# Both output projections of a two-block layer kernel turned token-major

## The chip, the cores and the metric

One core of one Trainium2 chip runs the whole program in one launch. The metric is the device time of that core in microseconds (us). The engines are TensorE (PE: matmuls, and its weight loads PEld), VectorE (DVE), ScalarE (ACT), GpSimd (POOL) and SyncE (SP), which issues nearly all transfers. P is 128, T (tokens) and D (features) are 1024, KT = TT = 8 tiles of 128, and HALF is 512.

## The reference, cut to what matters

Two transformer-like blocks follow each other. Block 1 ends in a gated residual and a final norm; block 2 norms its input, ends its mixer in a normed residual, and then runs a feed-forward part (FFN):

```
# block 1: merged is (T, D), the sum of three gated branches; gt_l comes from silu(c) @ w_ada + b_ada
x_new = x + gt_l * (merged @ w_out)
x2    = rmsnorm(x_new, final_g)                   # y * rsqrt(mean(y*y) + 1e-6) * g
# block 2
u  = rms_norm(x2, norm_mix_pre)                   # goes into the mixers (the first is hgrn)
h  = x2 + rms_norm(merged_2 @ w_out_2, norm_mix_post)
u  = rms_norm(h, norm_ffn_pre)
h  = h + rms_norm((silu(u @ w_gate) * (u @ w_up)) @ w_down, norm_ffn_post)
```

Everything is float32. Each product of the kernel is made of three matmuls of "high" and "low" parts: x = x_hi + x_lo with x_hi a rounded copy (fp32r), and x_hi w_hi + x_lo w_hi + x_hi w_lo is summed in PSUM.

## The kernel before, in words

**Feature-major sums.** Activations lie with features on the partitions: `h_hi`, `h_lo` and `acc` are [128, 8 feature tiles, 1024 tokens]. A product's output tile is 128 features by 512 tokens. Its stationary operand is a 128x128 block of the weights and its moving operand 512 tokens of `h`.

**Weights.** Weights arrive in chunks of 512 KB in two slots of `raw` (SP, `load_chunk`). ACT rounds a chunk into `w_hi` (`round_chunk`, L303), POOL subtracts to get `w_lo` (`rest_chunk`, L310), and `split` counts the halves that are ready. `used` counts chunks that PE has finished with.

**The merge ahead of each projection** writes the merged sum to `acc`, two feature tiles per turn of a loop, in the order 6, 7, 4, 5, 2, 3, 0, 1. PE makes a gate product and a branch product, ACT the sigmoid, DVE multiplies (L1197) and POOL adds into `acc` (L1166).

**`project_first` (L1558).** J = 16 pieces, each of one feature tile and one half of the tokens; the eight chunks of `w_out` are fetched twice, once for each half of the tokens. ACT and DVE first split the merged sum into high and low (L1622, L1667). For each piece PE turns four 128x128 blocks of x to feature-major (`turn`, L1743, from `res`, into which the merge loaded x), makes 24 matmuls, and DVE multiplies by the gate column `gate_t` and adds x (L1674). ACT squares twice (L1634, L1635), DVE sums the squares over the feature tiles (L1681), PE sums them over the partitions with one-column matmuls (`stats`, L1761), DVE and POOL make the two inverse roots (L1601), DVE writes a diagonal, and PE spreads it over the partitions (`spread`, L1769). The normed tiles (`normed`, L1706) are split again into `h_hi` and `h_lo`. x_new goes to DRAM (`keep`), and the inverse root of the first norm stays in `kept_rstd`.

**`project_second` (L1812)** does the same with `w_out_2`, but has two norms one behind the other (the product's, then the sum's), so it has four rounds of sum over partitions, inverse root and spread, and it first rescales the x_new that it has fetched back to get x2 (`rescale`, L1956). `add_residual` (L1838), `square_x` (L1901), `add_square_x` (L1978) and `weighted` (L1968) make the second norm.

**What follows.** Both end with `half_ahead`: products of the next stage's first two chunks with the first half of the tokens, 48 matmuls in four parts, between the last steps. The other half waits for `h_done`, the last `h_lo`. `ffn_and_output` (L3461) adds the residual at its end token-major, so PE turns `res` there (`residual_tile`, L3695) and ACT copies it (L3582). DVE adds the last products (L3621), POOL makes the inverse root (L3552), DVE scales (L3629) and DVE or POOL add the residual (L3511).

**What sets the order.** Each engine has its instructions in the order written, a queue of its own, and waits on semaphores between. Nothing is planned at run time. The same kind of product as the new one already stands in the FFN (`down_tile`, L3657 to L3659): a 128-token tile is stationary, a row of the weight matrix 512 wide moves, and the two output halves lie in different PSUM banks.

## Time and profile before

| | |
|---|---|
| three runs, us | 3081.94, 3085.1, 3087.03 (median 3085.1) |
| the profiled execution's own time, us | 3083.83 |
| its span in the profile, us | 3082.1 |
| PE busy | 2934.9 us, 95% of the span |
| DVE, ACT, POOL busy | 44%, 31%, 33% |
| mean granted TensorE clock | 0.979 |

The span runs from the program's first instruction to its last on the core. A busy matmul is not a matmul at its peak: their ends are modelled, and in a dense stream each overlaps the next, so the distance from start to start is what counts.

### The profile page before, as it was taken

Reading aid. Unit: us, or ns where it says so; the run is one execution under the profiler, and the core shown is the slowest. Engines: PE = TensorE matmul, PEld = TensorE weight load, DVE = VectorE, ACT = ScalarE, POOL = GpSimd, SP = SyncE. Lnnn points to the kernel's source line nnn. Section 1 sums busy time; section 2 is a strip of 40 time slices with the busy share of each in tenths; the row PEclk is TensorE's granted clock in tenths of the full one; section 3 lists DMA queues with packets and bytes.
Section 4 is the critical chain, followed back from the end, with each engine's and each line's share of the span. In section 5 each row is a group of like instructions: output and inputs, shape, how many; then the busy total and the mean of one; then the engine's idle time right before and its main releaser. Section 6 shows DMA issues by size and latency. Waiting matters only on the chain.

```text
span 3082.1 us, 40975 instructions
## 1 busy us (share of the span) xinstructions
PE 2934.9 (95%) x15675; PEld 2365.4 (77%) x15675; DVE 1352.4 (44%) x2203; ACT 956.7 (31%) x1574; POOL 1016.1 (33%) x801
## 2 busy tenths in 40 slices
PE   5999989999999999999989999989878999999998
PEld 3788778888888877788677888758666888888886
DVE  5244430111011035544379999850663324324325
ACT  4344532222233244332453222352332111111113
POOL 3534312233333345222122333304554223223223
PEclk8999999999999999999999999999988999999999
DMA  5211021111112122111011111102220111111111
GB/s 206 51 39 39 18 79 54 48 48 41 54 50 92 51 92 86 51 36 53 24 37 37 46 46 51 39 37 70 76 62 28 48 48 48 48 48 48 48 48 75
DMA packets 261468, 169.42 MB, mean 55 GB/s; under 512 B 23604, under 2 KB 250605, under 8 KB 260205
## 3 DMA queue, kind: packets, MB, share of 16 engines
q1 hardware_dynamic: 259997, 162.65, 17.5%
q10 hardware_dynamic: 1360, 5.24, 0.4%
q8 instruction: 75, 1.23, 0.2%
q14 instruction: 36, 0.29, 0.0%
HBM read 159.41 MB, written 8.45 MB: 54 GB/s over the span
## 4 chain that ended last, share of the span: by engine, by line
PE 87%; DVE 6%; issue 2%; ACT 2%; POOL 1%; DMA 1%; SPq 0%; POOLq 0%; DVEq 0%; ACTq 0%
PE ps L326 69%; PE ps L3658 3%; PE ps L3657 3%; PE ps L3659 2%; PE ps L983 1%; PE ps L997 1%; DVE score L3076 1%; DVE ssq L1944 1%; DVE h_lo L1934 1%; PE ps L2480 1%; PE ps L3402 1%; PE ps L3392 1%; DMA rows<-in_norm_ffn_post 0%; PE ps L969 0%; PE ps L1523 0%
## 5 line engine op out<-in xcount | busy, mean ns | idle before, releaser
L326 PE MATMUL ps<-h_hi,w_hi 128*128 128x512 f32 x2864 | 1139.1, 398 | 35.3 <-DVE h_lo L1934 10.1
L326 PE MATMUL ps<-h_lo,w_hi 128*128 128x512 f32 x2864 | 1123.3, 392 | 0.0
L326 PE MATMUL ps<-h_hi,w_lo 128*128 128x512 f32 x2864 | 1122.3, 392 | 0.0
L310 POOL TENSOR_TENSOR w_lo<-raw,w_hi 128x512 fp32r<-128x512 f32 (+2 forms) x556 | 658.2, 1205 | 1296.9 <-ACT w_hi L303 1296.7
L326 PEld LDWEIGHTS ps<-h_hi,w_hi 128*128 128x128 f32 x2864 | 542.2, 189 | 157.9 <-issue 19.6
L326 PEld LDWEIGHTS ps<-h_hi,w_lo 128*128 128x128 f32 x2864 | 542.0, 189 | 116.4
L326 PEld LDWEIGHTS ps<-h_lo,w_hi 128*128 128x128 f32 x2864 | 542.6, 189 | 111.0 <-issue 1.0
L303 ACT ACTIVATE w_hi<-raw 128x512 fp32r<-128x512 f32 (+2 forms) x556 | 288.3, 567 | 865.2 <-PE ps L326 701.5
L3607 DVE TENSOR_TENSOR act<-gate,ps 128x1024 f32<-128x1024 f32 x22 | 26.9, 1221 | 446.1 <-PE ps L326 446.1
L3616 DVE TENSOR_TENSOR acc<-acc,ps 128x1024 f32<-128x1024 f32 x160 | 195.4, 1221 | 28.6 <-PE ps L3659 28.6
L1197 DVE TENSOR_TENSOR part<-sig,ps 128x1024 f32<-128x1024 f32 x40 | 48.6, 1215 | 339.1 <-PE ps L326 285.5
L3168 DVE MATCH_REPLACE8 score<-best,score 128x384 f32<-128x384 f32 (+2 forms) x192 | 165.8, 876 | 0.0
L3169 DVE MAX8 best<-score 128x8 f32<-128x384 f32 (+2 forms) x192 | 155.7, 878 | 1.1
L3658 PE MATMUL ps<-w_lo,act_hi 128*128 128x512 f32 x352 | 140.3, 399 | 0.0
L3657 PE MATMUL ps<-w_hi,act_hi 128*128 128x512 f32 x352 | 139.4, 396 | 0.2 <-POOL w_lo L310 0.2
L3659 PE MATMUL ps<-w_hi,act_lo 128*128 128x512 f32 x352 | 138.1, 392 | 0.0
L3547 POOL TENSOR_TENSOR act_lo<-act,act_hi 128x1024 fp32r<-128x1024 f32 x21 | 50.6, 2408 | 187.2 <-ACT act_hi L3578 187.2
L1166 POOL TENSOR_TENSOR acc<-acc,part 128x1024 f32 x40 | 96.9, 2422 | 0.0
L3578 ACT ACTIVATE act_hi<-act 128x1024 fp32r<-128x1024 f32 x22 | 23.3, 1061 | 217.5 <-DVE act L3607 217.5
L3573 ACT ACTIVATE gate<-ps 128x1024 f32<-128x1024 f32 x22 | 22.6, 1027 | 211.1 <-PE ps L326 211.1
L3657 PEld LDWEIGHTS ps<-w_hi,act_hi 128*128 128x128 f32 x352 | 66.1, 188 | 17.2 <-POOL w_lo L310 0.6
L3659 PEld LDWEIGHTS ps<-w_hi,act_lo 128*128 128x128 f32 x352 | 66.1, 188 | 15.7
(434 smaller groups left out, 3406.5 us busy)
## 6 DMA issues: line engine op xcount, KB each, us to landing
raw<-in_w_in SPq DMA_DIRECT2D x88, 512.0 KB, 4.0
raw<-in_w_ffn_gate_up SPq DMA_DIRECT2D x44, 512.0 KB, 3.8
raw<-in_w_out SPq DMA_DIRECT2D x32, 512.0 KB, 3.7
raw<-in_w_gate SPq DMA_DIRECT2D x32, 512.0 KB, 4.1
raw<-in_w_ffn_down SPq DMA_DIRECT2D x22, 512.0 KB, 3.5
w_ada<-in_w_ada SPq DMA_DIRECT2D x8, 1024.0 KB, 10.7
x_tok<-in_x ACTq DMA_DIRECT2D x4, 1024.0 KB, 14.0
residual_gate<-in_w_ada SPq DMA_DIRECT2D x8, 512.0 KB
```

Of the source, the lines that this page charges most:

```text
L303: act.activation(w_hi[:, s, cut], raw[:, s, cut], ACT.Copy).then_inc(rounded.sem, 1)
L310: pool.tensor_tensor(w_lo[:, s, cut], raw[:, s, cut], w_hi[:, s, cut].bitcast(F32), ALU.subtract).then_inc(split.sem, 1)
L326: last = pe.matmul(dst, w[:, chunk[0] % 2, k], x(k), start=(k == ks[0] and n == 0), stop=(k == ks[-1] and n == 2))
L1166: pool.tensor_tensor(to, to, part[:], ALU.add).then_inc(o_evicted.sem, 1)
L1197: dve.tensor_tensor(part[:], sig[:, u % 2], ps[2 * (u % 2) + 1][:], ALU.mult)\
L3168: top_steps.done(dve.match_replace(part(b), best[:, j], part(b), TAKEN) if marking else dve.max(best[:, j], part(b)))
L3169: dve.max(best[:, j], part(b)))
L3547: pool.tensor_tensor(act_lo[:, f % 2], act32[:], act_hi[:, f % 2].bitcast(F32), ALU.subtract)\
L3616: dve.tensor_tensor(acc[:, t], acc[:, t], outs[t][:], ALU.add).then_inc(o_evicted.sem, 1)
L3657: pe.matmul(dst[:, c:c + HALF], act_hi[:, f % 2, tokens], w[0], start=first, stop=False)
L3658: pe.matmul(dst[:, c:c + HALF], act_hi[:, f % 2, tokens], w[1], start=False, stop=False)
L3659: last = pe.matmul(dst[:, c:c + HALF], act_lo[:, f % 2, tokens], w[0], start=False, stop=final)
```

## The change

`project_first` and `project_second` are written anew around one helper, `row_products`. The output tile is now 128 tokens by 1024 features (two banks of PSUM), the stationary operand a 128x128 block of the merged sum, the moving operand half a row block of the weight matrix. Norms, gains and residual then act on rows whose tokens lie on the partitions.

- **Weights:** `Rows` loads eight row blocks (128 rows of 4 KB) once, into `raw` and a second pair of slots, `raw_x`. Six of them are kept split in `rows_hi` and `rows_lo`. ACT rounds, and DVE, not POOL, subtracts.
- **Order:** token tiles 0 to 2 are worked on together, row block by row block in the order in which the merge finishes its tiles; the split of their 384 columns comes first (`first_tokens`), the other 640 later (`other_tokens`). Tiles 3 to 7 follow one by one, 48 matmuls each.
- **Per tile:** DVE `add`, a norm over the free axis (ACT square with its accumulator, DVE `mean`, POOL power, DVE `normed`), PE `turn` (eight 128x128 transposes into `ps3`), ACT `out_high`, DVE `out_low`.
- **Residual:** x comes token-major into the space of `acc` once that is split, in four parts of 1 MB. x2 itself (gain included) is stored and fetched back; `kept_rstd`, `rescale` and the FFN's `residual_tile` go.
- **Gate:** the gate of the residual is made as a row on all partitions (`gate_row`, two matmuls 512 wide in the first merge) instead of a column per feature tile.

The core of the diff:

```
+            def weights(self, m):
+                return [wide_row(x[:, m]) for x in (w_hi, w_lo)] if m < 2 else [self.high[:, m - 2], self.low[:, m - 2]]
+        def row_products(pe, rows, gates, turn, ahead, t_last=TT - 1):
+            def step(t, m, c, n, last=False):
+                x, w = ((h_hi, 0), (h_hi, 1), (h_lo, 0))[n]
+                return pe.matmul(ps[t % 3][:, c:c + HALF], tile_of(x, t)[:, ROW_ORDER[m]], rows.weights(m)[w][:, c:c + HALF],
+                                 start=(m == 0 and n == 0), stop=last and n == 2)
+            pe.wait_ge(*gates[1])
+            for m in range(6):
+                pe.wait_ge(hi_ready.sem, hi_ready.at(m + 1))
+                for t in range(FEW):
+                    for half, c in enumerate((0, HALF)):
+                        if t == 0:
+                            rows_ready(m, half)
+                        step(t, m, c, 0)
+                        step(t, m, c, 1)
+                pe.wait_ge(lo_ready.sem, lo_ready.at(m + 1))
+                for t in range(FEW):
+                    for c in (0, HALF):
+                        step(t, m, c, 2)
+            ...
+            for t in range(FEW, TT):
+                pe.wait_ge(evicted.sem, evicted.at(t - 2))
+                for m in range(KT):
+                    if m == 4 and t < 5:
+                        turn(2 * t - 6)
+                    for c in (0, HALF):
+                        for n in range(3):
+                            done = step(t, m, c, n, m == KT - 1)
+                ...
+                done.then_inc(o_ready.sem, 1)
+                turn(2 * t - 5 if t < 5 else t - 1)
+            pe.wait_ge(evicted.sem, evicted.at(TT - 1))
+            ahead(pe, KT, 0, 0)
+            ahead(pe, KT, 0, 1)
+            pe.wait_ge(evicted.sem, evicted.at(TT))
+            ahead(pe, KT, 1, 0)
+            turn(TT - 1)
+            ahead(pe, KT, 1, 1)
+        # project_first, ACT
+                    sum_high(act, rows, acc, tile_added)
+                    squares(0)
+                    squares(1)
+                    keep(0)
+                    squares(2)
+                    keep(1)
+                    keep(2)
+                    out_high(0)
+                    squares(3)
+                    out_high(1)
+                    ...
+                    for t in range(4, TT):
+                        squares(t)
+                        out_high(t - 1)
+                        if t == TT - 2:
+                            round_chunk(act, KT, 0, 0)
+                            round_chunk(act, KT + 1, 0, 0)
+                        keep(t)
+        # project_first, DVE
+                    def add(t):
+                        x, y = tmp[:, t % FEW], x_of(t)
+                        ...
+                        dve.tensor_tensor(x, ps[t % 3][:], gate_row[:], ALU.mult).then_inc(evicted.sem, 1)
+                        ...
+                        dve.tensor_tensor(x, x, y, ALU.add).then_inc(y_ready.sem, 1)
+                        ...
+                        dve.tensor_tensor(y, x, final_row[:], ALU.mult).then_inc(y_ready2.sem, 1)
+                    sum_low(dve, rows, acc)
+                    add(0)
+                    add(1)
+                    mean(0)
+                    normed(0)
+                    add(2)
+                    mean(1)
+                    normed(1)
+                    mean(2)
+                    normed(2)
+                    out_low(0)
+                    add(3)
+                    out_low(1)
+                    ...
+                    for t in range(4, TT):
+                        add(t)
+                        out_low(t - 1)
+                        mean(t)
+                        normed(t)
+                    out_low(TT - 1)
+        # PE, both projections
+                    def turn(t):
+                        pe.wait_ge(h_ready.sem, h_ready.at(t + 1))
+                        pe.wait_ge(o_evicted.sem, o_evicted.at(t))
+                        for k in range(KT):
+                            last = pe.transpose(ps[3][:, k * P:k * P + P], tmp[:, t % FEW, k * P:k * P + P], ident[:])
```

The hgrn stage now starts its first load ahead of its wait for `h_done`, and its POOL waits for the stored x2 before its first `rest_chunk`.

## Rows read from the trace of the kernel before

**Rows 1.** The page: the chain that ended last, share of the span by engine.

```profile
PE 87%; DVE 6%; issue 2%; ACT 2%; POOL 1%; DMA 1%; SPq 0%; POOLq 0%; DVEq 0%; ACTq 0%
```

**Rows 2.** Stretches: us; PE, PEld, DVE, ACT, POOL busy; clock; DMA share; GB/s.

```profile
1102.60:1232.00 129.40, 117.56 (x534) 94.88 (x532) 67.31 (x92) 60.03 (x109) 69.67 (x49) 0.96 0.30 96
2178.69:2342.66 163.97, 126.79 (x533) 100.60 (x533) 119.29 (x147) 55.85 (x99) 80.91 (x60) 0.87 0.20 58
```

**Rows 3.** Waits in 2160 to 2340 us: total us, times, longest.

```profile
PE ps L2057 <- DVE ssq_x L1978: 11.1, 1, 11.1
PE ps L326 <- DVE h_lo L1934: 10.1, 5, 4.9
```

**Rows 4.** PE in order of time: the first matmul behind each projection.

```profile
1232.00 0.77 PE L326 MATMUL ps<-h_hi,w_hi 128*128 128x512 f32 x1 [4.19 <-DVE h_lo L1582]
...
2342.66 0.76 PE L326 MATMUL ps<-h_hi,w_hi 128*128 128x512 f32 x1 [9.63 <-DVE h_lo L1832]
```

**Rows 5.** PE in order of time: dense streams, first and last matmul of each.

```profile
2196.09 0.39 PE L326 MATMUL ps<-h_hi,w_lo 128*128 128x512 f32 x1
...
2204.25 0.39 PE L326 MATMUL ps<-h_hi,w_lo 128*128 128x512 f32 x1
...
2343.22 0.63 PE L326 MATMUL ps<-h_lo,w_hi 128*128 128x512 f32 x1
...
2347.06 0.63 PE L326 MATMUL ps<-h_lo,w_hi 128*128 128x512 f32 x1
...
3007.74 0.39 PE L3657 MATMUL ps<-w_hi,act_hi 128*128 128x512 f32 x1
...
3015.45 0.39 PE L3657 MATMUL ps<-w_hi,act_hi 128*128 128x512 f32 x1
```

**Rows 6.** PE in order of time: eight transposes and the next matmul.

```profile
3047.31 1.03 PE L3695 MATMUL ps<-ident,res 128*128 128x128 f32 x8
3048.10 0.48 PE L3657 MATMUL ps<-w_hi,act_hi 128*128 128x512 f32 x1
```

**Rows 7.** DVE in order of time.

```profile
1102.88 1.22 DVE L1197 TENSOR_TENSOR part<-sig,ps 128x1024 f32<-128x1024 f32 x1 [15.28 <-PE ps L326]
1104.02 9.26 DVE L1667 TENSOR_TENSOR h_lo<-acc,h_hi 128x512 fp32r<-128x512 f32 x8
...
1115.25 0.68 DVE L1667 TENSOR_TENSOR h_lo<-acc,h_hi 128x512 fp32r<-128x512 f32 x1
...
2200.84 1.78 DVE L1934 TENSOR_TENSOR h_lo<-acc,h_hi 128x512 fp32r<-128x512 f32 x1
...
3049.45 1.28 DVE L3629 SCALAR_TENSOR_TENSOR acc<-acc,rstd,gate 128x1024 f32<-128x1024 f32 x1
...
3056.01 2.61 DVE L3629 SCALAR_TENSOR_TENSOR acc<-acc,rstd,gate 128x1024 f32<-128x1024 f32 x1
```

**Rows 8.** ACT in order of time.

```profile
1102.86 1.15 ACT L303 ACTIVATE w_hi<-raw 128x512 fp32r<-128x512 f32 x2 [0.25 <-PE ps L326]
...
3046.11 1.03 ACT L3582 ACTIVATE res<-ps 128x1024 f32<-128x1024 f32 x1 [2.73 <-PE ps L3695]
3047.03 1.05 ACT L3593 ACTIVATE act<-acc 128x1024 f32<-128x1024 f32 x1
3047.98 0.19 ACT L3593 ACTIVATION_READ_ACCUMULATOR act<-acc 128x1 f32 x1
```

**Rows 9.** POOL in order of time.

```profile
1104.72 2.83 POOL L1166 TENSOR_TENSOR acc<-acc,part 128x1024 f32 x1
...
2240.99 1.02 POOL L1853 TENSOR_TENSOR rs<-var,power 128x4 f32<-128x4 f32 x1 [6.35 <-DVE var L1961]
...
3054.63 0.54 POOL L3552 TENSOR_TENSOR rstd<-var,power 128x1 f32<-128x1 f32 x1 [1.94 <-DVE var L3625]
```

**Rows 10.** The page, DMA issues: count, KB each, us to landing.

```profile
raw<-in_w_out SPq DMA_DIRECT2D x32, 512.0 KB, 3.7
x_tok<-in_x ACTq DMA_DIRECT2D x4, 1024.0 KB, 14.0
```

More of the change, by code:

```diff
@@ L1240, in _ @@
                         pe.wait_ge(evicted2.sem, evicted2.at(U * N - 1))
-                        for d in range(KT):
-                            last = pe.matmul(ps[1][:, d:d + 1], residual_gate[:, 0, d * P:d * P + P], ones[:, 0:1],
-                                             start=True, stop=True)
+                        for c in (0, HALF):
+                            last = pe.matmul(ps[1][:, c:c + HALF], ones[:], residual_gate[:, 0, c:c + HALF], start=True, stop=True)
                         last.then_inc(sum_ready.sem, 1)
@@ new lines, in sum_low, with low @@
+        def sum_low(dve, rows, acc):
+            def low(cut, n, high_done, done):
+                dve.wait_ge(high_done.sem, high_done.at(n + 1))
+                dve.tensor_tensor(cut(h_lo, n), cut(acc, n), cut(h_hi, n).bitcast(F32), ALU.subtract).then_inc(done.sem, 1)
+            for n in range(KT):
+                low(first_tokens, n, hi_ready, lo_ready)
+                if n == 0:
+                    dve.wait_ge(split.sem, half_after(split, 0, 1, 0, 0))
+                if n < 2:
+                    rows.rest(dve, n + 1)
+                if n == 5:
+                    rows.rest(dve, 3)
+            rows.rest(dve, 4)
+            for m in range(5, KT):
+                rows.rest(dve, m)
+                for n in range(2 * (m - 5), 2 * (m - 5) + 2):
+                    low(other_tokens, n, y_hi, lo_ready2)
+            for n in range(6, KT):
+                low(other_tokens, n, y_hi, lo_ready2)
@@ new lines, in _ @@
+                @block.tensor
+                def _(pe):
+                    def turn(t):
[3 more added lines that the diff above has]
+                            last = pe.transpose(ps[3][:, k * P:k * P + P], tmp[:, t % FEW, k * P:k * P + P], ident[:])
+                        last.then_inc(transposed.sem, 1)
+                    row_products(pe, rows, gates, turn, half_ahead)
@@ new lines, in out_high @@
+                    def out_high(t):
+                        act.wait_ge(transposed.sem, transposed.at(t + 1))
+                        act.activation(tile_of(h_hi, t), by_feature(ps[3]), ACT.Copy).then_inc(y_ready3.sem, 1)
+                    sum_high(act, rows, acc, tile_added)
+                    square(0, 0)
+                    square(0, 1)
+                    square(1, 0)
+                    square(0, 2)
+                    square(1, 1)
+                    square(1, 2)
+                    out_high(0)
@@ L1930, in _ @@
+                    square(0, 3)
+                    out_high(1)
+                    square(1, 3)
+                    out_high(2)
+                    for t in range(4, TT):
+                        square(0, t)
+                        out_high(t - 1)
+                        square(1, t)
+                        if t == TT - 2:
+                            round_chunk(act, KT, 0, 0)
+                            round_chunk(act, KT + 1, 0, 0)
+                    out_high(TT - 1)
                 @block.vector
@@ L2016, in _ @@
+                    sum_low(dve, rows, acc)
+                    dve.wait_ge(side_loaded.sem, side_loaded.at(2))
+                    mean(0, 0)
+                    add(0)
+                    mean(0, 1)
+                    add(1)
+                    mean(1, 0)
                     normed(0)
+                    mean(0, 2)
+                    add(2)
+                    mean(1, 1)
                     normed(1)
-                    rest(dve, 1)
-                    evict(12)
+                    mean(1, 2)
@@ L2036, in _ @@
-                    for n in range(KT, J):
-                        normed(n)
-                        if n > KT and n % 2 == 0:
-                            rest(dve, n - 1)
-                    rest(dve, J - 1)
+                    out_low(0)
+                    mean(0, 3)
+                    add(3)
+                    out_low(1)
+                    mean(1, 3)
+                    normed(3)
+                    out_low(2)
+                    for t in range(4, TT):
+                        mean(0, t)
+                        add(t)
+                        out_low(t - 1)
+                        mean(1, t)
+                        normed(t)
@@ L2055, in stats @@
-                    def stats(src):
-                        for t in range(4):
-                            last = pe.matmul(ps[3][:, t:t + 1], src[:, t * P:t * P + P], ones[:, 0:1], start=True, stop=True)
-                        last.then_inc(scores.sem, 1)
-                    def spread(dst, n, scales):
-                        pe.wait_ge(biased.sem, biased.at(n + 1))
-                        pe.matmul(dst, ones[:], scales, start=True, stop=True).then_inc(pt_ready.sem, 1)
-                    pe.wait_ge(*gates[1])
```

830 lines of the change are left out of this document (300 added, 530 removed).

## The prediction

> **What bounds the kernel now.** I read the page's chain of waits first: PE holds 87% of it [rows 1], so what counts is where PE is idle, slow, or does work that the change drops. The two projections are stretches of their own in the view by windows. The first runs from 1102.60, where the merge's last product is issued, to 1232.00 us, the second from 2178.69 to 2342.66 [rows 2]. Their ends are the first matmuls that had waited for the last `h_lo` [rows 4]. Each stretch holds 384 matmuls of the projection and 48 of the next stage (`half_ahead`).
>
> A dense stream of such matmuls goes at (2204.25 - 2196.09) / 36 = 0.2267 us each [rows 5], so 432 need 97.9 us. The first projection takes 129.4 us, 31.5 over it, the second 164.0, 66.1 over it. The granted clock says the same: 0.96 and 0.87 [rows 2]. In the second, the view of waits names PE standing 11.1 us for the sum of the squares of h, and 10.1 us for splits of the merged sum, which DVE makes beside POOL [rows 3]. At its end there are two norms one behind the other, and the last wait alone is 9.63 us [rows 4]. The second stretch is where the money is.
>
> **The change part by part.** S is the moment when PE issues the first product of a projection.
>
> *Matmuls.* Their number stays: 8 token tiles x 8 row blocks x 2 halves x 3 = 384, and 48 ahead. Their pattern becomes that of `down_tile`: token tile stationary, weight row moving, the bank of PSUM changing every second or third matmul. There the step is (3015.45 - 3007.74) / 33 = 0.2336 us [rows 5]. The other end is 0.2267. I take 0.2336, the row of the same pattern: 432 x 0.2336 = 100.9 us.
>
> *Turns.* Eight turns of eight transposes take the place of one-column matmuls, spreads and, in the first projection, 16 turns of four. Eight transposes hold PE 0.79 us (3048.10 - 3047.31) [rows 6], and the next matmul starts some 0.1 late; I take 0.9, so 7.2 us. Sum per projection without a wait: 108.1 us.
>
> *The start.* Before, eight splits by DVE took 9.26 us [rows 7] and PE followed them one by one. Now PE has 108 matmuls (25.2 us) on tiles 6, 7, 4, 5, 2, 3 before it needs tiles 0 and 1. DVE is free at S + 1.5 (L1197 begins at S + 0.3 and takes 1.22 [rows 7]); then come the split of 384 columns (0.46, by 0.68 for 512) and row block 1 in two pieces of 0.6. POOL adds the last merged tile from S + 2.1 to S + 4.9 [rows 9], and DVE's two-input pieces in that time take 1.78 instead of 0.68 us [rows 7]. So block 1 is split at about S + 5.2, where PE wants its halves at S + 4.2 and S + 4.7: 0.4 us of wait. From then on POOL is idle. A block costs ACT 1.1 us [rows 8] and DVE 1.2, PE takes 4.2 over it. All of the splits, 1.2 for each block and 0.46 + 0.74 for each tile, end near S + 21.4, well before S + 34.0, when tile 3 starts. Blocks 2 to 7 arrive in 3.7 us each [rows 10], the last near S + 16, each issued as a slot comes free. In the second projection block 0 is ready only at about S + 0.3, and the waits of the start come to 0.5.
>
> *The middle, first projection.* Products 0 to 2 end at S + 28.4, 31.2 and 34.0. `add` is three ops of 1.22 with a hand-over, 3.86 us; a square with its accumulator is 1.05 + 0.19 [rows 8]; `mean` 0.3; the power lies between 0.54 (one column) and 1.02 (four) [rows 9], I take 0.7 for two; `normed` 1.28 [rows 7]. On DVE in the order written: add 0 and 1 until 36.3, normed 0 until 38.8, add 2 until 42.5, normed 1 until 45.0, normed 2 until 47.4. ACT has `keep(2)` ahead of `out_high(0)`, so that ends at 49.5 and `out_low(0)` at 50.7. But `turn(1)` needs `out_low(0)`, because there is one `ps3`, and PE arrives at 46.2, after tile 3. PE waits 4.6 us, and `turn(2)` another 0.8. Behind such a wait the clock is granted at half: 0.427 us a matmul against 0.2267, for 12 matmuls behind the wait of 9.63 us (9 steps of it in [rows 5]) and 7 behind that of 4.19. I add 7 x 0.2 = 1.4. From tile 4 on a tile is 11.2 + 0.9 us of PE against about 6.5 of DVE and 5.6 of ACT, so nothing waits.
>
> *The end, first projection.* Let T be when PE has issued the last product. From there: add 7 until T + 4.0; its second square until T + 5.2; `out_high(6)`, behind it on ACT, T + 6.3; `out_low(6)` T + 7.4; mean, power and `normed(7)` T + 10.0. PE meanwhile makes `turn(6)` and three of the four quarters ahead (0.9 + 8.4 = 9.3) and waits 0.7 for `turn(7)`. The last quarter (2.8) covers `out_high(7)` and `out_low(7)`. SP fetches the next two chunks right behind the fourth store of x2, and POOL's splits of them (2 x 2.55) lie ahead of its last power, which is needed later. Sum: 108.1 + 0.4 + 4.6 + 0.8 + 0.7 + 1.4 = 116.0 us, against 129.4. That is 13.4 saved, and 7 x 0.2 = 1.4 more, since hgrn no longer starts at half clock.
>
> *The second projection.* Both norms are chains of a square, `mean`, a power of 0.54 and one op, but `add` has two wide ops instead of three and nothing is kept, so `out_low(0)` ends at S + 47.7 where PE arrives at 46.2: 1.5 us. At the end `normed(7)` is done 8 us behind the last product and PE wants it after 9.3. Sum: 108.1 + 0.5 + 1.5 = 110.1 us against 164.0: 53.9 saved, and 12 x 0.2 = 2.4 for the FFN's first matmuls.
>
> *The FFN's end.* Eight turns leave PE and eight copies ACT. PE is not what is late there: DVE is busy from add to add, and the first square alone stands behind a copy of 1.03 us [rows 8], of which 0.6 is waiting. I take 0.6 (bounds 0 and 8 x 0.79 = 6.3).
>
> *At nothing:* the gate's row in the first merge (DVE has three more turns of that loop, 16 small matmuls become 2 wide ones); storing and fetching x2 in 4 MB each (the parts land from S + 20 on, the first is due at S + 29.7); hgrn's POOL waiting for the last store, which begins near S + 112 and has until S + 122. If a store or a part took 14.0 us like the four loads of x at the start [rows 10], x2's parts would come up to some 10 us late.
>
> Sum: 14.8 + 56.3 + 0.6 = 71.7. The profiled execution took 3083.83, which gives 3012.1; the median of the runs is 1.3 above it, so 3013.4.
>
> **Rules of the Trainium skill.** The row shows a split by DVE at 1.78 us beside POOL against 0.68 alone, and the scaling L3629 at 2.61 beside POOL's add against 1.28 [rows 7]. The Trainium skill, SBUF — State Buffer, section "Who interferes with whom", says that a VectorE instruction with two SBUF inputs blocks against a GpSimd instruction that reads SBUF. By it the splits of the weights, which were POOL's, cost DVE nothing beyond their own time, as POOL reads nothing wide after the merge's last add.
>
> **The rivals.**
> - *A second chain that paces PE* (waits in place of the sums over partitions). For it: turns are tied by one `ps3` and by the written order on ACT and DVE, and the middle already waits 4.6 us. Against it: from tile 4 on DVE has half of its time free. If hand-overs or the power cost twice what I take, each of the first turns and each end waits some 5 us more: 4 places, 20 us, 3033.
> - *Transfers late.* For it: row blocks pass through four slots, x through the space of `acc`, 14.0 us to land [rows 10]. Against: 3.7 us for the same 512 KB. 10 us: 3023.
> - *Slower than before: the half clock.* One mechanism: banks that change every two or three matmuls leave gaps in PE, the clock is granted at 1.2 GHz for both projections, and each of 768 matmuls costs 0.2 us more: 154 us, 3167. It decides from 0.09 us a matmul on, 71.7 / 768. Against: `down_tile` changes banks as often and keeps 0.2336 [rows 5], which only the 2.4 GHz level allows. [...]
> - *It doesn't do what it says:* the next stage gives it back, because its first tiles lie where the kept rows lay and it waits for them: within 0.2% of 3085.
>
> **How the numbers follow.** Forecast 3013, chance 0.76; its own range 3003 to 3023 (dense step 0.2267: - 4.6; no wait in the middle: - 6; other sizes of power and hand-over: + 8). Paced by the chain 0.11, late transfers 0.08, other partial loss 0.02, no change 0.01, half clock 0.02. Range 3001 to 3034. This kernel's runs agree within 0.2%, some 6 us, and anything inside that is "same". Faster 0.96, same 0.01, slower 0.03.
>
> **What would show it.** Right: the stretches take about 116 and 110 us at a clock near 1.0; the new matmuls stand 0.23 us apart; `h_lo` no longer releases PE at a start; one wait of some 5 us at the second turn of the first projection and 1 to 2 us in the second; no half-clock matmuls at hgrn's or the FFN's start. Wrong: PE waiting at turns from tile 4 on, DVE pieces of 1.7 us after S + 5, PE waiting for weight rows, steps of 0.43 us.

## The result and the profile after

The changed kernel takes 3011.65 us (median of 4 runs, 3009.72 to 3013.24) against 3083.52 us before (4 runs, 3080.61 to 3087.03) on the same chip: ratio 0.9766, 95% interval 0.9749 to 0.9783. The forecast was 3013 us, with a range of 3001 to 3034. The profiled execution's span is 3007.9 us (before 3082.1) at a mean clock of 0.988 (0.979).

The page's chain by engine answers to [rows 1]: PE now holds 89% of it. The two stretches, with the same columns, answer to [rows 2]:

```profile
PE 89%; DVE 5%; ACT 2%; issue 2%; POOL 1%; DMA 1%; SPq 0%; POOLq 0%; DVEq 0%; ACTq 0%
```

```profile
1102.75:1219.77 117.02, 110.60 (x497) 89.79 (x496) 74.23 (x87) 51.06 (x76) 15.22 (x20) 0.97 0.33 115
2161.20:2270.90 109.70, 108.25 (x497) 87.48 (x497) 63.76 (x79) 45.09 (x75) 18.74 (x26) 1.00 0.28 96
```

The first projection went from 129.4 to 117.0 us, the second from 164.0 to 109.7, and the second now runs at a mean clock of 1.00. The waits of PE in the changed kernel, first from 1085 to 1225 us and then from 2160 to 2300 us (total us, times, longest), answer to [rows 3]. What stood at 11.1 and 10.1 us is gone, and only five single waits are left:

```profile
PE ps L1864 <- DVE h_lo L1830: 4.4, 1, 4.4
PE ps L1864 <- DVE tmp L1825: 1.3, 1, 1.3
PE ps L1651 <- DVE w_lo L1589: 0.7, 1, 0.7
...
PE ps L2035 <- DVE h_lo L1997: 1.1, 1, 1.1
PE ps L1651 <- DVE w_lo L1589: 0.3, 1, 0.3
```

L1651 is the new product, L1864 and L2035 are the turns, L1589 DVE's split of the row blocks. The largest wait is the one in the middle of the first projection. PE in order of time around it, and what DVE and ACT did for it:

```profile
1149.09 0.39 PE L1651 MATMUL ps<-rows_hi,h_lo 128*128 128x512 f32 x1
1153.90 1.94 PE L1864 MATMUL ps<-ident,tmp 128*128 128x128 f32 x8 [4.42 <-DVE h_lo L1830]
1155.49 0.78 PE L1651 MATMUL ps<-w_hi,h_hi 128*128 128x512 f32 x1
1156.07 0.63 PE L1651 MATMUL ps<-w_lo,h_hi 128*128 128x512 f32 x1
...
1159.48 0.44 PE L1651 MATMUL ps<-w_hi,h_hi 128*128 128x512 f32 x1
```

```profile
1140.66 1.29 DVE L1825 SCALAR_TENSOR_TENSOR tmp<-acc,rstd,pre_row 128x1024 f32<-128x1024 f32 x1 [0.89 <-POOL rstd L1748]
1152.53 1.23 DVE L1830 TENSOR_TENSOR h_lo<-ps,h_hi 128x1024 fp32r<-128x1024 f32 x1 [2.12 <-ACT h_hi L1777]
```

```profile
1150.44 1.15 ACT L1773 ACTIVATE acc<-acc,rstd 128x1024 f32<-128x1024 f32 x1 [1.21 <-DVE tmp L1825]
1151.49 1.00 ACT L1777 ACTIVATE h_hi<-ps 128x1024 fp32r<-128x1024 f32 x1
```

Tile 0 is normed at 1141.95, PE turns it, but ACT reads the turned tile only at 1151.49, behind the `keep` of tile 2 (L1773), and DVE follows at 1152.53. The second turn writes to the same PSUM buffer, `ps3`, and stands for 4.42 us. Behind it the eight transposes are spread over 1.94 us instead of 1.03, and of the nine matmuls up to 1159.05 the next stands 0.58 us away once and 0.43 us eight times, which is the 1.2 GHz level.

Where the 74.2 us between the two spans went, from distances between the same places in both traces. A projection counts here from the moment when PE has issued the merge's last product:

| stretch | before, us | after, us |
|---|---|---|
| first projection | 129.4 | 117.0 |
| from it to the second | 946.7 | 941.5 |
| second projection | 164.0 | 109.6 |
| FFN, to the end | 739.4 | 737.0 |

In the second projection PE's waits came to 37.2 us before and to 1.4 after, and 38 matmuls stood 0.43 us apart before, one after. So some 43 of its 54 us are waits and the half clock behind them; the rest lies in the smaller matmuls and between them. PE hardly waited for the splits of the weights before (0.3 us in the second projection, nothing in the first), so waiting for weights that were fetched twice is not what the change took away.

### The profile page after: what moved, and what is told of

It is laid out like the page before. It is cut to its first block, busy times and chain, and to the rows that moved or that the text cites. A ratio compares the mean times of both kernels' runs of the same rounds, so it can differ in the third digit from the quotient of the medians.

```text
span 3007.9 us, 40407 instructions
## 1 busy us (share of the span) xinstructions
PE 2898.8 (96%) x15527; PEld 2336.7 (78%) x15527; DVE 1304.3 (43%) x2130; ACT 928.4 (31%) x1510; POOL 898.9 (30%) x737
## 4 chain that ended last, share of the span: by engine, by line
PE 89%; DVE 5%; ACT 2%; issue 2%; POOL 1%; DMA 1%; SPq 0%; POOLq 0%; DVEq 0%; ACTq 0%
PE ps L326 67%; PE ps L1651 5%; PE ps L3582 3%; PE ps L3584 3%; PE ps L3583 3%; PE ps L983 1%; PE ps L997 1%; DVE score L3013 1%; PE ps L2417 1%; PE ps L3339 1%; PE ps L3329 1%; DMA rows<-in_norm_ffn_post 0%; PE ps L969 0%; PE ps L1523 0%; PE ps L3350 0%
## 5 line engine op out<-in xcount | busy, mean ns | idle before, releaser
L326 PE MATMUL ps<-h_hi,w_hi 128*128 128x512 f32 x2608 | 1027.9, 394 | 4.7 <-POOL w_lo L310 4.7
L326 PE MATMUL ps<-h_hi,w_lo 128*128 128x512 f32 x2608 | 1017.2, 390 | 0.0
L326 PE MATMUL ps<-h_lo,w_hi 128*128 128x512 f32 x2608 | 1016.8, 390 | 0.0
L310 POOL TENSOR_TENSOR w_lo<-raw,w_hi 128x512 fp32r<-128x512 f32 (+1 forms) x496 | 567.5, 1166 | 1199.1 <-ACT w_hi L303 1199.1
L326 PEld LDWEIGHTS ps<-h_hi,w_hi 128*128 128x128 f32 x2608 | 490.4, 188 | 109.2 <-POOL w_lo L310 5.3
L326 PEld LDWEIGHTS ps<-h_hi,w_lo 128*128 128x128 f32 x2608 | 490.1, 188 | 103.9
L326 PEld LDWEIGHTS ps<-h_lo,w_hi 128*128 128x128 f32 x2608 | 490.7, 188 | 100.6 <-issue 0.2
L303 ACT ACTIVATE w_hi<-raw 128x512 fp32r<-128x512 f32 (+1 forms) x496 | 253.9, 561 | 861.4 <-PE ps L326 695.8
```

What stands on the lines that cost most here:

```text
L303: act.activation(w_hi[:, s, cut], raw[:, s, cut], ACT.Copy).then_inc(rounded.sem, 1)
L310: pool.tensor_tensor(w_lo[:, s, cut], raw[:, s, cut], w_hi[:, s, cut].bitcast(F32), ALU.subtract).then_inc(split.sem, 1)
L326: last = pe.matmul(dst, w[:, chunk[0] % 2, k], x(k), start=(k == ks[0] and n == 0), stop=(k == ks[-1] and n == 2))
```

## The experiments

Each comparison is with the kernel before on the same chip, whose median lay between 3080.9 and 3083.0 us. Two of the kernels below join one new projection to the old other one. Block 2's residual is then read in a form that the other stage doesn't write; apart from one memset that sets the old factor to 1, the instructions are those of the two parents.

### The two projections apart

`e_first`: the new first projection, with the old second and the old FFN end. `e_second`: the reverse.

```
 e_first:   merge, project_first, hgrn of after; project_second and the FFN's end of before
 e_second:  merge, project_first, hgrn of before; project_second and the FFN's end of after
```

> The new first projection alone; the second projection and the FFN's end are the old ones. The factor by which the old second projection brings x_new to x2 is set to 1, and x2 lies token-major where it expects feature-major, so only times are meant. Theory (each projection's gain is its own: fewer waits of PE at its start and end): the kernel before less 12.2 us of the stretch and 1.4 us of half clock at hgrn's start, some 3070 us, or 3066 if the 3.5 us of a landing in the memory stage come too. Rival (the gains need each other, since the old second projection rescales what the first has kept): 3083 or above.

Measured: 3061.53 us (3060.39 to 3062.19), ratio 0.9928 (0.9912 to 0.9943).

> The old first projection, the new second one and the new end of the FFN. The old first stores x_new feature-major and the new second takes it as x2 token-major, without the first norm's factor and gain, so only times are meant. Theory: less 54.3 us of the stretch and 2.3 us of half clock at the FFN's start, 3083.5 - 56.7 = 3026.8 us, its stretch 109 to 111 us. Rival (half of the second's gain comes from the first's part, x2 being kept instead of x_new): about 3055.

Measured: 3024.49 us (3020.30 to 3028.53), ratio 0.9805 (0.9786 to 0.9823). From the second projection's first product to the FFN's first down product it took 142.34 us, against 142.22 in the changed kernel and 199.13 before.

The second projection came out as expected: its stretch took 109.8 us. The four executions of `e_second` lie in two pairs, near 3020.6 and 3028.3 us, and the traced one is of the upper pair.

`e_first` gained more (21 us) than its projection accounts for: from the first product to hgrn's state products it took 206.5 us against 221.0 before, 14.5 less. Of the 22.2 us between the two spans another 1.6 are the first 98 us of the program, which take 95.6 to 98.3 us in the traces, whatever the kernel, and 3.6 lie at one chunk of the memory attention. The theory had those 3.6 in its second number, 3066, and the measured time is 4.5 us below even that.

The two gains apart, 21.0 and 58.0 us, add up to 79, where both changes together gave 72. The memory attention is faster in both traces (by 3.6 and 2.7 us), which counts it twice; the rest isn't settled, and is of the size by which executions differ. Neither projection needs the other's change for its gain.

### The order of `out_high` and `out_low`

`e_order` moves the two ops that read a turned tile ahead of work on later tiles, for tiles 0 to 2 of the first projection and for tile 0 of the second:

```
 # project_first, ACT                 # DVE
   keep(0)                              add(2)
+  out_high(0)                       +  out_low(0)
   squares(2)                           mean(1)
   keep(1)                              normed(1)
+  out_high(1)                          ...
   keep(2)                              normed(2)
-  out_high(0)                       -  out_low(0)
   squares(3)                        +  out_low(1)
-  out_high(1)                          add(3)
+  out_high(2)                       -  out_low(1)
   keep(3)                              ...
-  out_high(2)
```

> The new kernel with another written order in the middle of both projections: out_high(0) and out_low(0) come right behind the first turn, ahead of the squares and the keep of later tiles. Nothing is left out. Theory (the wait of 4.4 us at the second turn is the written order of ACT and DVE, not their load): the wait of the first projection falls below 1 us, with it 9 matmuls and one turn at half clock (2.5 us), and 1.1 us of the second projection: 3011.7 - 7.5 = 3004 us. Rival (DVE's load through three tiles sets it; then the wait comes back at turn 2 or 3): at most 3 us gained, 3009.

Measured: 3000.08 us (2995.29 to 3002.18), ratio 0.9729 (0.9714 to 0.9744), below the changed kernel's interval. The first projection of its trace, and DVE's two ops on turned tiles:

```profile
1100.91:1210.63 109.72, 107.72 (x497) 87.66 (x496) 74.08 (x87) 51.14 (x76) 15.21 (x20) 1.00 0.34 123
```

```profile
1143.71 1.22 DVE L1830 TENSOR_TENSOR h_lo<-ps,h_hi 128x1024 fp32r<-128x1024 f32 x1
1149.58 1.22 DVE L1830 TENSOR_TENSOR h_lo<-ps,h_hi 128x1024 fp32r<-128x1024 f32 x1
```

`out_low(0)` stands 42.8 us behind the stretch's start instead of 49.8. The stretch has 109.7 us against 117.0, at clock 1.00 against 0.97. Its 7.3 us are the wait of 4.4, the transposes and the first matmul behind it (1.59 + 0.58 instead of 0.79 + 0.32, so 1.1), and eight steps of 0.43 instead of 0.23 (1.6), 7.1 in all. The wait of 1.1 us in the second is gone too. So the order written on ACT and DVE was the cause, not a lack of time on either. The theory had 7.5 us in all, and the ratio fell by 11 us' worth; the trace is 13.5 us shorter, of which some 5 lie outside the projections, 1.8 of them in the first 98 us of the program, 2.4 between the projections and 0.7 at the FFN's end. None of that is code that `e_order` changes.

### Three tiles one by one

`e_alone` does tiles 0 to 2 each with 48 matmuls in a row, where the changed kernel goes row block by row block over all three:

```
-            for m in range(6):
-                ...
-                for t in range(FEW):
-                    for half, c in enumerate((0, HALF)):
+            for t in range(FEW):
+                for m in range(KT):
+                    if t == 0:
+                        pe.wait_ge(hi_ready.sem, hi_ready.at(m + 1))
+                        pe.wait_ge(lo_ready.sem, lo_ready.at(m + 1))
```

> The new kernel, but token tiles 0 to 2 are worked on one behind the other from the start, so PE needs all eight row blocks within the first tile. Nothing is left out. Theory (working on three tiles together is what hides the arrival, rounding and splitting of the row blocks): the eighth block is ready about 20 us after the start, so tile 0 ends near S + 22 and tile 2 near S + 43.5 in place of S + 33.4; 10 us and some half clock in each projection, 3032 to 3036 us. Rival (the start is cheap either way, since DVE splits without POOL beside it): under 5 us lost, 3016.

Measured: 3017.86 us (3014.97 to 3019.48), ratio 0.9786 (0.9770 to 0.9803). My theory missed: the loss against the changed kernel (0.9766 and 0.9759 in two series) is 6 to 8 us, and the rival's 3016 was nearer. The intervals of the ratios overlap, so the loss rests on the traces: 1.3 us more from the first projection to hgrn's state products, 7.4 more from the second to the FFN's first down product. Its waits (total, times, longest), first projection and then second:

```profile
PE ps L1651 <- DVE h_lo L1629: 2.1, 1, 2.1
PE ps L1651 <- DVE rows_lo L1589: 1.9, 2, 1.0
PE ps L1854 <- DVE tmp L1815: 1.3, 1, 1.3
PE ps L1651 <- ACT h_hi L1607: 1.1, 1, 1.1
PE ps L1854 <- DVE h_lo L1820: 0.7, 1, 0.7
...
PE ps L1651 <- DVE rows_lo L1589: 2.5, 2, 1.3
PE ps L1651 <- ACT h_hi L1607: 2.1, 1, 2.1
PE ps L1651 <- DVE h_lo L1629: 1.7, 1, 1.7
```

The waits at the start did come, 5.1 and 6.3 us of them, but four in each projection, and from there on the blocks are ahead of PE. And in the first projection most of it was paid back: tile 0 is finished earlier, so the wait in the middle shrank from 4.4 to 0.7 us. Taking three tiles together is worth 6 to 9 us, not some 20.

### Who splits the row blocks

`e_pool` gives the splits of row blocks 1 to 7 to POOL in both projections:

```
 # DVE, sum_low                           # POOL
-                rows.rest(dve, n + 1)    +  for m in range(1, KT):
-            rows.rest(dve, 4)            +      rows.rest(pool, m)
             ...                             pool.wait_ge(hi_ready.sem, hi_ready.at(KT))
-                rows.rest(dve, m)
```

> Changed: in both projections POOL and not DVE splits row blocks 1 to 7 (14 pieces of 128x512, 1.3 us each by its rows elsewhere). Theory (POOL's merge add is what holds DVE at the start, and only there; DVE is the right engine for these splits): POOL can begin block 1 only behind its last merge add, at S + 4.9, and needs 2.6 us for it, so PE stands some 3 us longer at the start of each projection (first wait about 3.5 us instead of 0.74), and some half clock behind it: 3012 + 6 to 9 = 3018 to 3021. DVE's own pieces of h up to S + 26 cost more than their 0.46 us alone. Rival (DVE's share of the splits is what delays the start; on POOL they are free): the start waits disappear, 3009 to 3011.

Measured: 3015.70 us (3011.84 to 3016.38), ratio 0.9783 (0.9768 to 0.9798). PE's waits for the row blocks, first and second projection:

```profile
PE ps L1645 <- POOL w_lo L1589: 2.9, 2, 2.2
...
PE ps L1645 <- POOL w_lo L1589: 2.4, 2, 1.6
```

DVE's splits of the merged sum in the first projection (ns min/median/max, first and last start, form): two before POOL's last add begins, six of the same 384 columns beside POOL's merge add and splits, eight of 640 columns beside its splits. Then POOL's own splits in that time:

```profile
L1629 DVE TENSOR_TENSOR h_lo<-acc,h_hi x2: 551/552/553, 1104.1 to 1104.6; 128x384 fp32r<-128x384 f32 x2
...
L1629 DVE TENSOR_TENSOR h_lo<-acc,h_hi x6: 1617/1638/2780, 1105.0 to 1114.0; 128x384 fp32r<-128x384 f32 x6
...
L1629 DVE TENSOR_TENSOR h_lo<-acc,h_hi x8: 1573/1908/1914, 1115.9 to 1128.3; 128x640 fp32r<-128x640 f32 x8
...
L1589 POOL TENSOR_TENSOR rows_lo<-raw_x,rows_hi x4: 1598/1600/1604, 1110.5 to 1115.1; 128x512 fp32r<-128x512 f32 x4
```

The waits rose from 0.7 to 2.9 and from 0.3 to 2.4 us, less than the 3 us each that the theory said but of its sign, so the rival falls. The times alone say it less clearly, since the intervals of the two ratios overlap. In the changed kernel, where POOL is idle behind the merge's last add, the same splits are short:

```profile
L1629 DVE TENSOR_TENSOR h_lo<-acc,h_hi x8: 543/546/551, 1104.2 to 1113.3; 128x384 fp32r<-128x384 f32 x8
...
L1629 DVE TENSOR_TENSOR h_lo<-acc,h_hi x8: 809/811/812, 1116.2 to 1123.7; 128x640 fp32r<-128x640 f32 x8
```

So the slowing lasts as long as POOL works, and it is no fixed factor: a DVE split beside POOL took about as long as POOL's instruction, 2.78 us beside the merge's add of 2.74, 1.62 beside splits of 1.60, and 1.91 beside splits of 1.88. The factor is 5 in the first case, 3 in the second and 2.4 in the third. POOL's own splits grew too, from 1.30 us in the merge. The Trainium skill, SBUF — State Buffer, section "Who interferes with whom", has the rule that a VectorE instruction with two SBUF inputs contends with a GpSimd instruction that reads SBUF; the trace agrees, with 1.62 us beside POOL against 0.55 without it.

### The FFN's end

From the last three gate and up matmuls to the end it is 44.82 us before, and 44.88 after: removing the turns brought nothing. In the changed kernel PE comes to the last down chunk early and waits 2.04 us for its split. `e_turns` puts 16 transposes back into that place, whose results nobody reads. `e_tail` instead has ACT round that chunk one step earlier:

```
 e_turns, PE                                        e_tail, ACT
+ pe.wait_ge(evicted.sem, evicted.at(FT))          +     if f == FT - 1:
+ for d in range(KT):                              +         round_chunk(act, 3, 0, 4)
+     pe.transpose(ps[0][...], xt[:, 0, ...], ...)       act.wait_ge(h_ready.sem, ...)
+ ... (the same into ps[1])                              ...
  split_ready(pe, 2, 0, 4)                           def end():
                                                   -     round_chunk(act, 3, 0, 4)
```

> Changed: 16 transposes whose results nobody reads stand at the FFN's end ahead of the last down chunk, as the turns of two tiles did before; ACT's copies stay away. Theory (PE stood there anyway): they lie in the wait, which falls from 2.04 to about 0.4 us, the half-clock matmuls behind it go, and the span stays within 1 us of 3007.9. Rival (turns on PE cost their own time): the span is 1.6 us longer and the wait stays.

> Changed: in the last section of the FFN, ACT rounds the last down chunk ahead of its last act_hi, not behind it. Theory (the removed turns only laid bare a wait of PE for the last down chunk's w_lo, 2.04 us, and 8 matmuls at half clock behind it, 1.6 us): the wait and the half clock go, some 3 us of it reach the end: 3008.5 to 3009. Rival (DVE's chain from add to add sets the end, and act_hi is now later): no gain, 3011 to 3013.

Measured: `e_turns` 3007.19 us in its one run (a span of 3005.4), `e_tail` 3007.89 us (3001.46 to 3008.39), ratio 0.9754 (0.9740 to 0.9768), which overlaps the changed kernel's interval. PE in order of time at the last down chunks, of the changed kernel, of `e_turns`, of `e_tail`:

```profile
2968.72 0.80 PE L3582 MATMUL ps<-w_hi,act_hi 128*128 128x512 f32 x1 [2.04 <-POOL w_lo L310]
2969.32 0.63 PE L3583 MATMUL ps<-w_lo,act_hi 128*128 128x512 f32 x1
```

```profile
2963.41 1.09 PE L3624 MATMUL ps<-ident,acc 128*128 128x128 f32 x8 [0.50 <-DVE act L3532]
2968.16 0.50 PE L3582 MATMUL ps<-w_hi,act_hi 128*128 128x512 f32 x1 [0.15 <-POOL w_lo L310]
```

```profile
2968.69 0.48 PE L3583 MATMUL ps<-w_hi,act_hi 128*128 128x512 f32 x1 [1.76 <-DVE act_lo L3560]
```

In `e_turns` the wait fell to 0.15 us and the half clock behind it is gone, while the end still lies 44.19 us behind the last gate and up product. Unchanged code gave 44.15 (`e_order`, `e_pool`) to 44.88 us, by whether the matmuls behind the wait ran at half clock, so the turns had been free. `e_tail` has 43.32 us: 1.5 us less than the changed kernel's trace, half of what the theory said, and 0.8 less than the traces whose matmuls ran at full clock there. The next wait, for `act_lo`, takes the place of the first at 1.76 us.

### Where the operands lie

The step from one 128x512 matmul to the next was the term of the prediction that weighed most (432 x 0.2336 in each projection). The trace of after shows both levels within one tile, whose pattern of banks does not change. In tile 6 of the first projection the moving operand is first `w_hi` or `w_lo` and then `rows_hi` or `rows_lo`:

```profile
1182.88 0.39 PE L1651 MATMUL ps<-w_hi,h_lo 128*128 128x512 f32 x1
...
1184.92 0.39 PE L1651 MATMUL ps<-w_hi,h_lo 128*128 128x512 f32 x1
...
1185.61 0.39 PE L1651 MATMUL ps<-rows_hi,h_lo 128*128 128x512 f32 x1
...
1193.34 0.39 PE L1651 MATMUL ps<-rows_hi,h_lo 128*128 128x512 f32 x1
```

That is 2.04 / 9 = 0.2267 and 7.73 / 33 = 0.2342 us. Two kernels change nothing but addresses (a filler of 32 bytes moves up what the stages allocate; the other moves `h_hi` and `h_lo` to the upper end of SBUF and the stages' buffers 64 KB down):

```
 e_align:          lb = sb(ctx, "lb", [P, 8])
                 + filler = sb(ctx, "filler", [P, 8])
 e_high:         - h_hi = sb(ctx, "h_hi", [P, KT, T], F32R)
                 + h_hi = sb(ctx, "h_hi", [P, KT, T], F32R, side="right")     (h_lo too)
```

> Changed: one buffer of 32 bytes that nobody uses stands between the kernel's lasting buffers and those of the stages, so that the latter begin 32 bytes higher. Found in the trace of the changed kernel: matmuls of 128x512 stand 0.2273 us apart where both operands begin at a multiple of 64 bytes (w_hi, w_lo, h_hi, h_lo) and 0.234 where one of them begins 32 bytes off it (rows_hi and rows_lo, y_hi_t and y_lo_t, act_hi and act_lo), whatever the pattern of banks. Theory (the offset is the cause): 576 + 576 + 1056 = 2208 such matmuls go to 0.2273, 2208 x 0.0067 = 14.8 us less, 2997; ya, yb, yc and ym, which are allocated from the other side and keep their offset, stay at 0.234; the small matmuls of hgrn, whose buffers lose their alignment, may give back a little. Rival (the step belongs to the pattern of banks or to what the operands are): every step stays, 3012.

> Changed: h_hi and h_lo are allocated from the upper end of SBUF (163808 and up), so that every stage's buffers move down by 64 KB (rows_hi begins at 43296, y_hi_t too, act_hi at 138208); nothing else. e_align left every 0.234 us step where it was, so the offset in 64 bytes isn't the cause. Theory (it is where an operand lies: so far all that lay below 106624 goes at 0.2273 and all that lay above at 0.234): the 7824 matmuls of h_hi and h_lo with w_hi and w_lo go to 0.234, 7824 x 0.0067 = 52 us more, a span of 3060, and those of y_hi_t, now low, go to 0.2273. Rival (it is what the operands are, or how they are traversed): all steps stay, 3008 to 3010.

Measured: `e_align` 3004.45 us (3001.11 to 3005.00), ratio 0.9747 (0.9733 to 0.9760). `e_high` 3054.07 us in its one run, a span of 3052.3. The mean distance in us from such a matmul to the next, by the pair of operands (steps over 0.3 us left out), with the addresses at which the two begin in the changed kernel (the first of each name; the second projection's `rows_hi` begins at 170976):

| operands | begin at | after | e_align | e_high |
|---|---|---|---|---|
| w, h (L326) | 24704, 41088 | 0.2273 | 0.2273 | 0.2335 |
| rows, h (L1651) | 108832, 41088 | 0.2338 | 0.2332 | 0.2282 |
| y_hi_t, y_lo_t, w | 108832, 24704 | 0.2340 | 0.2333 | 0.2341 |
| act, w | 203744, 24704 | 0.2342 | 0.2325 | 0.2340 |

And three of the matmuls of `e_high` in the same tile, the last `w` matmul 9 behind the first row and 36 ahead of the last:

```profile
1200.29 0.40 PE L1651 MATMUL ps<-w_hi,h_lo 128*128 128x512 f32 x1
...
1202.40 0.39 PE L1651 MATMUL ps<-w_hi,h_lo 128*128 128x512 f32 x1
...
1210.64 0.39 PE L1651 MATMUL ps<-rows_hi,h_lo 128*128 128x512 f32 x1
```

`e_align` refuted the theory of the 64 bytes: no step went to 0.2273, they fell by 0.0006 to 0.0017, and the interval overlaps the changed kernel's. `e_high` refuted its rival, that the step belongs to what the operands are: w with h now stands 0.2335 us apart (here 2.11 / 9 = 0.2344), and rows with h fell to 0.2282 (here 8.24 / 36 = 0.2289). 7824 x 0.0062 less 576 x 0.0056 is 45.3 us, and the span grew by 44.4. But its theory, everything below 106624 fast, falls as well: y_hi_t and w both lay low there and kept 0.234. What is shown is that the step, within 3%, goes by the addresses of the two operands. Which relation between them decides stays open. That both begin at the same remainder to 64 bytes would fit `e_high`, where rows and h both begin 32 bytes off a multiple of 64 and are fast, and w lies on one and h off it and are slow. It doesn't fit `e_align`, where all of them begin at multiples of 64 and three pairs keep 0.2325 to 0.2333.

### The memory attention, and one execution against another

Between the projections 5.2 us went. 1.4 are hgrn's start at full clock. 3.6 lie at one wait, for the fourth and last chunk of `w_mem_kv`: 3.45 us of waiting before and 0.99 after, and half clock behind it before. `before_again` and `after_again` are the two kernels once more.

> The kernel before, unchanged, for a second trace of it. Between the projections the changed kernel was 5.2 us shorter, 3.6 of it at one weight chunk of the memory attention, and e_second, whose first projection is the old one, had 2.7 of that too. Theory (the 3.6 us is how that transfer happened to land in the one profile of before): here PE's wait at that chunk is near 1 us, and the stretch from the indexer's last product to the memory attention's v_t some 26.5 us instead of 30.1. Rival (it belongs to the kernel): 3.5 us again.

> The changed kernel, unchanged, beside the others on one chip: 3009 to 3012. Its second trace shows how much of the differences between kernels in single stretches (2 us in the first 98 us, up to 5 us in the sparse attention) comes from one execution to the next.

Measured: `before_again` 3081.47 us in its one run, `after_again` 3009.06 us (3003.87 to 3010.01), ratio 0.9759 (0.9745 to 0.9773). The stretch from the turn of the memory to the turn of v took 30.06 and 29.98 us before, 26.48 and 26.57 after. My theory of chance fell; it belongs to the kernel. ACT at that chunk, of before and of after, and the DMA view of the few us around it, again of before and of after:

```profile
1588.54 1.15 ACT L303 ACTIVATE w_hi<-raw 128x512 fp32r<-128x512 f32 x2 [6.06 <-DMA raw<-in_w_mem_kv]
```

```profile
1572.34 1.15 ACT L303 ACTIVATE w_hi<-raw 128x512 fp32r<-128x512 f32 x2 [3.69 <-DMA raw<-in_w_mem_kv]
```

```profile
q8 instruction: 1, 0.02, 2.4%
...
raw<-in_w_mem_kv SPq DMA_DIRECT2D x1, 512.0 KB, 6.1
```

```profile
raw<-in_w_mem_kv SPq DMA_DIRECT2D x1, 512.0 KB, 3.7
```

In both traces of before a transfer of the queue named "instruction" stands beside the chunk, which lands in 6.1 and 5.8 us. In `e_second`, whose program is the old one up to there, it does too: 4.6 us. In the other eleven traces, all with the new first projection, none stands there, and the chunk lands in 3.6 to 3.9 us. That is a match in fourteen traces and not a cause: in the same eleven such a transfer stands beside the second chunk of `w_mem_kv` instead, which lands in 3.6 to 4.0 us all the same. The changed kernel's, as an example:

```profile
q14 instruction: 2, 0.02, 1.3%
...
raw<-in_w_mem_kv SPq DMA_DIRECT2D x1, 512.0 KB, 3.8
```

So why the last chunk lands late with the old first projection stays open.

The two traces of the changed kernel agree from 547 us on in every stretch to within 0.2 us, but others of the same code differ. The sparse attention takes from 91.3 us (`before_again`) to 97.4 us (`e_second`) in the fourteen traces, as here of the changed kernel and of `e_tail` (columns of [rows 2]):

```profile
1957.31:2049.77 92.46, 78.38 (x433) 50.96 (x432) 64.71 (x148) 58.16 (x125) 2.67 (x3) 0.93 0.03 8
```

```profile
1953.78:2050.04 96.26, 82.34 (x433) 53.16 (x432) 64.61 (x148) 58.20 (x125) 2.68 (x3) 0.88 0.03 7
```

The matmuls are the same and the waits within 0.2 us of each other, and it takes 3.8 us more at a lower clock. So differences of a few us between kernels in a stretch with waits are not to be read as the kernels'.

### All together

`best2` has the order of `e_order`, the earlier rounding of `e_tail`, and fillers of 32 bytes at both ends of SBUF.

> All that gained so far together: out_high and out_low of a tile as soon as its norm is there (as in e_order, ratio 0.9729 to the kernel before), the last down chunk rounded earlier (as in e_tail, 1.6 us in the FFN), and the stages' buffers at multiples of 64 bytes, now from both sides (as in e_align). Expected by the sum of what their traces show in their own stretches: 3000 - 1.6 - 1.9 = 2996.5. If the 64 bytes do nothing at all: 2998.5. It should beat both kernels.

Measured: 2996.94 us (2993.22 to 3000.75), ratio 0.9723 (0.9709 to 0.9738). It beats the kernel before and, run with it, the changed one (0.9759, 0.9745 to 0.9773). From `e_order` alone (0.9729) it can't be told by time. Its trace shows 43.26 us at the FFN's end as in `e_tail`, and the `ya`, `yb`, `yc` and `ym` products at 0.230 instead of 0.234.

## Why the prediction was right

The time, 3013 against 3011.65, and the mechanism were right: the gain is PE's waits and the half clock behind them, and most of it lies in the second projection. The profiled spans differ by 74.2 us where the sum said 71.7. That the time came out within 1.4 us is in part luck, since the five executions of `after_again` alone spread over 6 us, and errors of opposite sign below cancel in part.

- **Second projection:** 110.1 us forecast, 109.7 measured. Start 0.3 (0.5 forecast), `turn(1)` 1.1 (1.5).
- **First projection:** 116.0 forecast, 117.0 measured. The middle wait is 4.42 us (4.6) for the reason given: `keep(2)` ahead of `out_high(0)`, one `ps3`. `turn(2)` did not wait (0.8 forecast), since the half clock had delayed PE. Half clock: nine matmuls and a stretched turn, 2.7 us, against 1.4; I had counted the matmuls by the smaller case of [rows 4] and forgotten that transposes slow down too. Start 0.74 (0.4), `turn(7)` 1.26 (0.7).
- **The dense step:** 0.2336 was the right value for 288 of 432 matmuls, by luck and for the wrong reason. I took it as that of the pattern of banks, and the pattern doesn't make it: 96 matmuls of the same pattern, those with `w_hi` or `w_lo`, had 0.229 in the mean and 0.227 in the median. Dense matmuls come to 288 x 0.2338 + 96 x 0.2290 + 48 x 0.2273 = 100.2 us, against 100.9. The range's 4.6 us for a step of 0.2267 should have been 864 x 0.0069 = 6.0.
- **Turns:** 0.79 us and the next matmul 0.09 late, as taken.
- **DVE beside POOL:** the effect was right and its size read from the wrong row. The 1.78 us of [rows 7] is a split beside a POOL split of 1.75 us; beside the merge's add, which is what overlaps here, a split of the kernel before took 2.87 us. In the changed kernel block 1's first piece took 0.68 us and the second, beside that add of 2.86 us, 2.90, so the block was ready at S + 5.4 instead of S + 5.2, with S as in the prediction (ns min/median/max):

```profile
L1589 DVE TENSOR_TENSOR w_lo<-raw,w_hi x2: 685/1792/2898, 1104.6 to 1105.2; 128x512 fp32r<-128x512 f32 x2
```

- **No half clock at the next stages:** hgrn's first matmuls stand 0.23 us apart from 1219.77 on, the FFN's from 2270.91 on, so 1.4 and 2.4 us came as forecast.
- **FFN's end:** 0.6 us forecast, none came. The turns had lain in a wait; without them the wait is 2.04 us.
- **Not foreseen:** 3.6 us in the memory attention, whose cause is open. The sum promised 1.0 us too much in the first projection and 0.6 in the FFN, and this one outweighs both; without it the spans would differ by 70.6 us.

Of the rivals, pacing by the second chain didn't occur: from tile 4 on no turn but the last waits. No transfer was late: PE waited for none, and the page has 3.5 us for the row blocks, where [rows 10] had 3.7. The half clock by changes of bank did not occur: in both projections the bank changes at every third matmul or more often, at clocks of 0.97 and 1.00, and without the middle wait the first has 1.00 too (`e_order`). The Trainium skill, TensorE: Matmul & The Clock Gate, section "A second HAM failure mode: psum-queue depth-cycling", tells of a bf16 kernel that goes through the PSUM banks, whose PE idled briefly between groups of matmuls and whose clock went to and fro between its two levels. The traces here show no such thing: the second projection goes through its banks for 384 matmuls at a clock of 1.00.

## What to carry to other kernels

A sum over partitions is worth replacing by a turn to token-major even though the turn costs PE 0.9 us a tile: the gain is mostly waits, not matmuls saved (66 us over the dense time in one projection, 12 after; 43 of the 54 us are waits and half clock). When one PSUM buffer passes tiles from PE to two other engines, put the ops that empty it ahead of work on later tiles: that alone was 7.3 us here where the wait itself was 4.4, because the clock falls behind it. An op taken out of a place where its engine waits anyway gives nothing, so look first at what is late next.

## What the runs showed of the hardware

- The distance between dense 128x512 matmuls has levels 3% apart that go by where the two operands lie: moving `h_hi` and `h_lo` alone cost 44 us (`e_high`).
- Whether the clock falls behind a wait varies: the same 2.04 us wait at the FFN's end was followed by matmuls at half clock in both traces of the changed kernel (steps of 0.43 us) and at full clock in `e_order`, whose code there is the same.

```profile
2955.91 0.50 PE L3582 MATMUL ps<-w_hi,act_hi 128*128 128x512 f32 x1 [2.04 <-POOL w_lo L310]
2956.25 0.40 PE L3583 MATMUL ps<-w_lo,act_hi 128*128 128x512 f32 x1
```

- A DVE op with two SBUF inputs took as long as the POOL instruction beside it: 0.55 us alone, 1.62 beside POOL splits of 1.60 (`e_pool`); 0.68 alone, 2.90 beside POOL's add of 2.86 (the changed kernel).
- A transfer of the instruction queue beside a weight chunk of 512 KB doesn't by itself make it late. Over the fourteen traces 407 chunks had one beside them and landed in a median of 4.1 us (3.4 to 11.6), 2525 had none and landed in 3.8 (3.3 to 11.7).
